# Channel normalisation behind a depthwise convolution: three of eight chunks move from VectorE to GpSimd

## The reference

```python
def layer_norm(x, g, b):                      # over the 1024 channels of one token
    mu = jnp.mean(xf, axis=-1, keepdims=True)
    xc = xf - mu
    y = xc * lax.rsqrt(jnp.mean(xc * xc, axis=-1, keepdims=True) + LN_EPS)
    return (y * g + b)

def conv_module(xn, conv_state, w_pw1, b_pw1, w_dw, b_dw, ln_g, ln_b, w_pw2, b_pw2):
    ...                                       # pointwise D->2D, GLU: u
    dw = lax.conv_general_dilated(u_ext, w_dw, ...) + b_dw      # depthwise, width 31
    z = jax.nn.silu(layer_norm(dw, ln_g, ln_b))
    return z @ w_pw2 + b_pw2, last_rows(u_ext, CONV_STATE)
```

## Time and profile before

| what | value |
|---|---|
| median of 3 runs | 1355.87 us (1353.28 to 1357.66) |
| the profiled execution's own time | 1352.04 us |
| span of the profiled execution | 1350.4 us |
| busy in the span | PE 1082.7 us (80%), DVE 491.2 (36%), ACT 305.0 (23%), POOL 208.2 (15%) |
| mean granted TensorE clock | 0.9 of full speed |

### The profile page before, as it was taken

One profiled execution on the slowest core, in us unless ns is written; L12 is line 12 of the kernel. 1 busy time (PEld: TensorE's weight loads), 2 busy tenths in 40 slices (PEclk: granted clock), 3 DMA queues, 4 the chain that ended last, 5 costly groups with the idle time before them and its releaser, 6 DMA issues.

```text
span 1350.4 us, 14690 instructions
## 1 busy us (share of the span) xinstructions
PE 1082.7 (80%) x5162; PEld 609.6 (45%) x5162; DVE 491.2 (36%) x1062; ACT 305.0 (23%) x628; POOL 208.2 (15%) x223
## 2 busy tenths in 40 slices
PE   6999999988984987777752999988885977788870
PEld 5777777764443332222312777643443322233320
DVE  3244334442436111111116499984445111111115
ACT  3223232322101111111003355543111111111002
POOL 2000000001014000000011288850004000000003
PEclk9999999988985998889885999998886999988895
DMA  8833333616116899999966922100027999999956
GB/s 284 253 104 104 103 103 101 215 53 262 56 63 235 339 422 422 422 422 422 421 244 196 352 64 65 28 24 0 22 90 264 406 423 423 423 423 422 422 226 241
DMA packets 106911, 322.87 MB, mean 239 GB/s; under 512 B 12635, under 2 KB 59867, under 8 KB 81881
## 3 DMA queue, kind: packets, MB, share of 16 engines
q1 hardware_dynamic: 94569, 288.30, 54.8%
q0 software_dynamic: 12304, 34.09, 7.1%
HBM read 270.48 MB, written 61.84 MB: 246 GB/s over the span
## 4 chain that ended last, share of the span: by engine, by line
PE 48%; DMA 27%; DVE 11%; issue 11%; ACT 2%; POOL 1%; SPq 1%; DVEq 0%; POOLq 0%
DMA ring<-in_w_up 24%; PE bank L1078 12%; PE bank L486 10%; PE bank L403 7%; PE bank L513 4%; DVE bank L1534 2%; PE bank L536 2%; PE bank L1095 2%; PE bank L552 2%; PE bank L577 2%; PE bank L411 1%; PE bank L328 1%; PE bank L899 1%; DMA ring<-in_w_qkv 1%; PE bank L1367 1%
## 5 line engine op out<-in xcount | busy, mean ns | idle before, releaser
L1078 PE MATMUL bank<-ring,work 128*64 128x512 f32 x1056 | 273.2, 677 | 75.4 <-DMA ring<-in_w_up 72.3
L1078 PEld LDWEIGHTS bank<-ring,work 128*64 128x64 f32 x1056 | 88.8, 155 | 257.3 <-issue 218.4
L1095 PE MATMUL bank<-ring,work 128*64 128x512 f32 x528 | 120.6, 598 | 25.3 <-DVE work L1114 25.3
L1110 DVE TENSOR_TENSOR work<-work,bank 128x256 f32<-128x256 f32 x33 | 13.9, 421 | 337.1 <-ACT work L1106 337.1
L1350 PE MATMUL bank<-xt_flat,work 128*128 128x288 f32 x512 | 128.7, 413 | 5.0 <-DVE work L1515 3.4
L486 PE MATMUL bank<-xt_flat,ring 128*128 128x288 f32 x512 | 131.9, 412 | 0.6 <-issue 0.6
L403 PE MATMUL bank<-ring,xn_flat 128*128 128x512 f32 x256 | 121.3, 628 | 7.4 <-ACT xn_flat L1465 6.6
L1350 PEld LDWEIGHTS bank<-xt_flat,work 128*128 128x128 f32 x512 | 98.2, 193 | 35.2 <-DVE work L1515 3.1
L1481 POOL TENSOR_TENSOR ring<-ring 128x606 f32<-128x606 f32 x76 | 103.8, 1366 | 63.6 <-ACT ring L1430 53.9
L486 PEld LDWEIGHTS bank<-xt_flat,ring 128*128 128x128 f32 x512 | 94.9, 190 | 33.2 <-issue 8.5
L1534 DVE SCALAR_TENSOR_TENSOR bank<-work,ring,bank 128x606 f32<-128x606 f32 x129 | 98.9, 847 | 0.0
(11 more groups left out here) (242 smaller groups left out, 1100.2 us busy)
## 6 DMA issues: line engine op xcount, KB each, us to landing
ring<-in_w_gate SPq DMA_DIRECT2D x32, 2048.0 KB, 20.3
ring<-in_w_up SPq DMA_DIRECT2D x32, 2048.0 KB, 24.8
ring<-in_w_down SPq DMA_DIRECT2D x32, 2048.0 KB, 25.0
work<-x_sorted SPq DMA_DIRECT2D x33, 512.0 KB, 10.4
ring<-in_w_qkv SPq DMA_DIRECT2D x24, 512.0 KB, 6.0
x_sorted<-gain POOLq DMA_DIRECT2D x8, 1536.0 KB, 5.8
y_sorted<-work SPq DMA_DIRECT2D x17, 512.0 KB, 24.3
y_sorted<-gain SPq DMA_DIRECT2D x16, 512.0 KB, 25.2
```

The lines of the kernel that those rows point to most:

```text
L1078: mm = nc.tensor.matmul(bank[2 + s][rr, :], xte[s][:, c, rr], wgu[s][:, :, e, c, :], start=c == 0, stop=c == C - 1)
L1095: mm = nc.tensor.matmul(bank[5 + h][rr, :], hts[:, c, rr], wdn[s][:, e, c, h * HALF:(h + 1) * HALF], start=c == 0, stop=c == FC - 1)
```

## The change

The mean is copied from PSUM to SBUF (into `prod[0]`, which is free by then), by VectorE. Chunks 3, 5 and 7 are then centred and later scaled by GpSimd, each in one instruction of 576 columns; VectorE keeps chunks 0, 1, 2, 4 and 6. ScalarE waits for each chunk on the semaphore of the engine that made it, in the same order of chunks as before. VectorE tells GpSimd by two further counts of `conv_done`: one behind the copy, one behind the reciprocal (a `sem_inc` of its own).

```diff
+        mean_sb = prod[0][:, 0:TOKENS]
+
+        def wait_chunk(eng, by_vector, c, phase):
+            if c in POOL_CHUNKS:
+                eng.wait_ge(side_done, SIDE_LEAD + SIDE * (C - 1) + LAST_SIDE - 1 + len(POOL_CHUNKS) * phase + POOL_CHUNKS.index(c) + 1)
+            else:
+                eng.wait_ge(by_vector, VECTOR_CHUNKS.index(c) + 1)
 ...
@@ conv_act
             for c in range(C):
-                act.wait_ge(centred, c + 1)
+                wait_chunk(act, centred, c, 0)
                 nc.scalar.activation(sq[:, c, :], dw[:, c, :], ACT.Square).then_inc(sq_done, 1)
 ...
             for c in range(C):
-                act.wait_ge(scaled, c + 1)
+                wait_chunk(act, scaled, c, 1)
                 nc.scalar.activation(dw[:, c, :], dw[:, c, :], ACT.Silu, ...).then_inc(swished, 1)
 
+        POOL_CHUNKS = (3, 5, 7)
+        VECTOR_CHUNKS = tuple(c for c in range(C) if c not in POOL_CHUNKS)
@@ conv_pool, behind its last chunk
+            pool.wait_ge(conv_done, C + CONV_LEAD + 1)
+            for c in POOL_CHUNKS:
+                pool.tensor_tensor(dw[:, c, :], dw[:, c, :], mean_sb, ALU.subtract).then_inc(side_done, 1)
+            pool.wait_ge(conv_done, C + CONV_LEAD + 2)
+            pool.wait_ge(sq_done, C)
+            for c in POOL_CHUNKS:
+                pool.tensor_tensor(dw[:, c, :], dw[:, c, :], sig[:], ALU.mult).then_inc(side_done, 1)
@@ conv_dve
             dve.wait_ge(mean_mm, 2)
-            for c in range(C):
+            V.tensor_copy(mean_sb[:, 0:SEQ], bank[0][:])
+            V.tensor_copy(mean_sb[:, SEQ:TOKENS], bank[1][:, 0:DEC]).then_inc(conv_done, 1)
+            for c in VECTOR_CHUNKS:
                 V.tensor_tensor(dw[:, c, 0:SEQ], dw[:, c, 0:SEQ], bank[0][:], ALU.subtract)
                 V.tensor_tensor(dw[:, c, SEQ:TOKENS], dw[:, c, SEQ:TOKENS], bank[1][:, 0:DEC], ALU.subtract).then_inc(centred, 1)
             dve.wait_ge(std_done, 1)
             steps.done(V.reciprocal(sig[:], sig[:]))
-            for c in range(C):
+            dve.sem_inc(conv_done, 1)
+            for c in VECTOR_CHUNKS:
                 V.tensor_tensor(dw[:, c, :], dw[:, c, :], sig[:], ALU.mult).then_inc(scaled, 1)
```

## The result

The changed kernel takes 1357.60 us (median of 20 runs), the kernel before 1354.78 us (20 runs): ratio 1.0019, 95% interval 1.0010 to 1.0028, or 2.6 us slower (1.4 to 3.8); the two medians themselves lie 2.8 us apart. A second timing of the same kernel gave 1.0024 (1.0012 to 1.0036). That is inside the forecast range and inside 0.3%, but clear of zero, and it isn't the +0.13 us that I took as likeliest.

What follows compares the result with a forecast made beforehand. TensorE was taken as the slowest consumer in centring and scaling, with only VectorE's first chunk waited for. Terms 0 + 0 + 0.13 + 0 = +0.13 us on 1355.87 gave 1356.0 us, range 1352.5 to 1360.5.

Steps and rivals of the forecast that it cites:

- forecast range: Whole kernel: 1352.5 to 1360.5 us around the forecast median of 1356.0 us.
- +0.13 us: Whole kernel, likeliest case: all moved work stays hidden and only the count behind the reciprocal costs; chance 0.52.
- The two copies, cost 0: Ahead of the centring: VectorE's copies of the mean take 0.73 us, hidden because ScalarE is still busy; slack 0.28 us.
- Three centrings at 1.30 us (1.19 to 1.52), cost 0: Centring phase: GpSimd has chunks 3, 5 and 7 ready before ScalarE's turn for them; cost 0, gain 0.
- The count, 0.13 us: Between reciprocal and first scaling: a separate semaphore instruction on the chain adds 0.13 us, bounds 0 and 0.17.
- Three scalings, cost 0: Scaling phase: GpSimd has chunks 3, 5 and 7 ready before ScalarE comes to them; cost 0, gain 0.
- Rival A: Scaling phase: VectorE and GpSimd take turns, VectorE first; +0.5 to +1.5 us, say +1.0, giving 1356.9; chance 0.35.
- GpSimd takes the first turn: +2.8 us: Scaling phase, engines taking turns: chunk 0 comes 1.30 us late and all behind it; 1358.7 us.
- Rival B: Both phases: GpSimd instructions cost far more on these tiles; at 4 us each +6.7 us, 1362.6; chance 0.07.
- Rival C: Both phases: VectorE's relief of 3.5 us reaches the end, giving 1352.4 us; chance 0.03.
- rival A's dear end: Scaling phase: engines take turns with GpSimd first; counted as 2.7 us in the range's upper limit of 1360.5.
- Same: Whole kernel: time within 0.3% of the kernel before; chance 0.88, against faster 0.03 and slower 0.09.

Runs made afterwards that it cites:

- centring only: The changed kernel with all eight scalings left on VectorE and no count behind the reciprocal; ratio 0.9999 to the kernel before.
- idle writes: The kernel before plus the count behind the reciprocal and three GpSimd memsets of 576 columns on an unneeded buffer; one execution, scaling stretch 14.73 us against 14.82.
- VectorE first: The changed kernel with the count that releases GpSimd's scalings moved behind VectorE's first scaling; ratio 0.9992 to the kernel before.

## Why the prediction was right or wrong

- *The two copies, cost 0: right.* 0.69 and 0.21 us, hidden by L1463 as by L1455 before; centring only measured 0.9999.
- *Three centrings at 1.30 us (1.19 to 1.52), cost 0: right.* 4.14 us for three, 1.38 each. VectorE beside them has one input in PSUM and keeps its 0.73 us.
- *The count, 0.13 us: right.* 0.12 in the run with idle writes.
- *Three scalings, cost 0: wrong, and this is the step that failed.* The likeliest case put the overlap of the two engines at nothing. I laid GpSimd's 1.30 us and VectorE's 0.67 beside each other as if independent. They excluded each other. The Trainium skill's rule (SBUF — State Buffer, "Who interferes with whom") that I had quoted against the change is what happened, and the traces agree with it in its two halves: a VectorE instruction with two SBUF inputs is held up by, or holds up, a GpSimd instruction that reads SBUF (VectorE 1.99 for 0.75, GpSimd 1.91 for 1.40), while neither a second input in PSUM (0.75) nor a GpSimd instruction that only writes (0.75) does so.
- *Rival A had the mechanism; its chance, 0.35, was too low,* and I gave the first turn to VectorE. The variant "GpSimd takes the first turn: +2.8 us" is the one that came: 1.35 us of late start (0.13 of it the count), about 0.3 of waits for chunks and about 0.7 of a later rise of the clock make 2.34, and 0.56 more by the end of the projection, 2.90. It begins first by 0.02 us, since the count that releases it stands ahead of VectorE's instruction.
- *Rival B, a dear GpSimd instruction: no.* 1.38 to 1.92 us, waits included, against the 2.84 and 2.92 from which it would have cost time. *Rival C, relief that reaches the end: no.* VectorE left centring early, and the square root came when it came before.
- *The range held,* because rival A's dear end was in it, and not by the mechanism that I took as likeliest. "Same" by 0.3% was right in size; the sum of +0.13 was short by about 2.5 us. That 1357.60 lies only 1.6 us over the forecast 1356.0 is in part luck: the forecast stood on a median of three runs, 1355.87, and twenty gave 1354.78.

Open: the clock's rise. The late start explains 1.35 us of the first half's delay for certain. With an early start the rise came 3.6 to 4.5 us behind it in six traces; with a late one at 5.8, 5.9 and 6.2 in three and at 2.8 and 3.1 in two. Counted from the end of the variance instead, it came at 10.3 to 11.1 us in eight of these traces and at 13.7 to 13.9 in the three; so a start at 7.7 to 7.9 us is seen with either, and what decides between them no run shows.

## What to carry to other kernels

Before moving elementwise work to GpSimd, look at what VectorE runs beside it: in these runs an operand in PSUM made the overlap free, with both in SBUF the two engines took turns, and only an instruction beside such a partner shows it. If they must overlap, release GpSimd behind VectorE's first instruction and not ahead of it: that one line was worth the whole loss here, as far as the timing can tell (0.9992, 0.9978 to 1.0005). And when a stage has one producer and a slower consumer, only the first piece is on the chain; cut that piece smaller (by the consumer's tile, 0.40% here) rather than give later pieces away.

## What the runs showed of the hardware

- VectorE with two SBUF inputs and GpSimd reading SBUF alternated instruction by instruction, in all three rounds of the changed kernel, with ends 0.61 and 1.26 us apart, and their recorded durations include the wait.
- VectorE's instruction that only counts a semaphore did not wait for the end of the scaling ahead of it, in the run with VectorE first: GpSimd's instruction is recorded from 0.11 us behind the start of the VectorE scaling that preceded the count, 0.65 us ahead of its end.
- ScalarE's table load stood directly ahead of the first instruction that needs it: a copy put ahead of the first Silu moved a load of 1.28 us from under the reciprocal onto the chain.
